# Hybrid state-space and attention encoder on one core: sine arguments in the front, scan outputs through ScalarE, scan input products in pairs

## The chip, the cores and the metric
One core of a Trainium2 chip runs the whole program in one launch. The metric is device time in microseconds. The kernel before takes 1440.96 us, the median of 3 runs (1439.4 to 1441.56).

## What is computed
Two layers over 256 tokens of width 1024, all in float32:

```python
h = rmsnorm(x, g_mix); u, q, k, v = split(h @ w_in)
y_ssm = ssm_mixer(u)          # bidirectional complex-diagonal scan, GELU, GLU, norm
y_att = diff_attention(q, k, v)   # 4 heads, two softmax maps per head
x = x + concat(y_ssm, y_att) @ w_out
h = rmsnorm(x, g_ffn)
x = x + swiglu(h)             # layer 0: dense; layer 1: top 2 of 8 experts
```

The scan part: 32 channel groups with 64 complex states each, forward and backward. A state update is `s[t] = lam * s[t-1] + b(u[t])` with complex `lam`; the output is the real part of `C s`.

## The kernel before
A layer is a front (norm, projection of `u`, tables of the scan), 22 steps in which the scan and the attention run side by side, and an end (gates, output projection, norm). Then come the weights' passes: dense in layer 0, the experts in layer 1, streamed from HBM.

**The scan.** Each of 16 steps i handles two channel groups on 128 partitions. The complex decay is split: its size goes into a real scan, its angle into a rotation before and one after. TensorE makes the input products (`bu`, L1883 to L1892: four products with 64 rows each, rows 0 to 63 for even steps and 64 to 127 for odd ones) into a PSUM bank. VectorE rotates them by cosines and sines (`rotate_in`, L1300 and L1302; `add_in`, L1309) and scans (L1321). GpSimd rotates back (three operations, L646 to L651, into `ro`, two steps deep) and TensorE sums over the states (`outputs`, L1905 to L1924, once for two steps) into `ps[:, 2 + ft % 2]`. Four steps fill one such sum.

**Angles.** ScalarE multiplies positions by the turn of a step and, for the cosine, adds a quarter (`phases`, L729 and L730, four activations of 128 columns); adds a large constant to round (`nearest`, L739); VectorE subtracts the whole turns (`fracs`, L1274); ScalarE takes three sines (`trigs`, L746 to L750). This is done for each step, two steps ahead. `trig` is three steps deep and freed by GpSimd (`products`).

**GELU.** VectorE copies a finished sum, squares, scales and multiplies it (`gelu_in`, L1281 to L1284), ScalarE takes tanh (L756), VectorE closes (`gelu_out`, L1289), reading the sum in PSUM.

**Attention.** Head h starts at step 6, 8, 10, 12. At its step TensorE makes two score maps; one step later VectorE takes minima over rows and scales them (`score`, L1331 and L1332) and ScalarE takes the exponentials with their sums (L768). Two steps later VectorE takes reciprocals (`sums`, L1338 and L1339), ahead of that step's rotation. Three steps later ScalarE puts them on diagonals (L779) and at step +4 TensorE turns the maps (L1956); at +5 it makes the head's output (L1963), which ScalarE empties (L789, L790). Head pairs are normed on VectorE (`head_norm`, L1345 and L1346) and then projected (L1978).

**Order.** Each engine's list is written out by hand per step. TensorE in step i: `bu(i+1)`, the projections of q, k, v (L1863 at steps 0, 1, 3, 4; L2016 at 6 and 8), the attention work, then `outputs`. ScalarE in step i: phases of i+2, sines of i+1, emptying, attention, tanh. Sine, exponential with tanh, and square root need different activation tables, loaded by `ACT_TABLE_LOAD`.

## Time and profile before

| | |
|---|---|
| median of 3 runs | 1440.96 us |
| span of the profiled execution | 1437.0 us (no other time is given for it) |
| TensorE busy | 1348.0 us (94%) |
| VectorE busy | 875.8 us (61%) |
| ScalarE busy | 694.7 us (48%) |
| GpSimd busy | 135.4 us (9%) |

Layer 0's mixer runs from the start to about 200 us, its dense part to 387 us, layer 1's mixer to about 574 us, the experts to the end. A timeline line gives start, length, engine, line of the kernel, operation, tiles and shapes, and in brackets the idle time before it with what ended it. A TensorE product in float32 has two records.

### The profile page before, as it was taken

Reading aid. Unit: us, or ns where it says so; the run is one execution under the profiler, and the core shown is the slowest. Engines: PE = TensorE matmul, PEld = TensorE weight load, DVE = VectorE, ACT = ScalarE, POOL = GpSimd, SP = SyncE. Lnnn points to the kernel's source line nnn. Section 1 sums busy time; section 2 is a strip of 40 time slices with the busy share of each in tenths; the row PEclk is TensorE's granted clock in tenths of the full one; section 3 lists DMA queues with packets and bytes.
Section 4 is the critical chain, followed back from the end, with each engine's and each line's share of the span. In section 5 each row is a group of like instructions: output and inputs, shape, how many; then the busy total and the mean of one; then the engine's idle time right before and its main releaser. Section 6 shows DMA issues by size and latency. Waiting matters only on the chain.

```text
span 1437.0 us, 19125 instructions
## 1 busy us (share of the span) xinstructions
PE 1348.0 (94%) x7246; PEld 980.9 (68%) x7246; DVE 875.8 (61%) x1138; ACT 694.7 (48%) x1023; POOL 135.4 (9%) x111
## 2 busy tenths in 40 slices
PE   6996889999899779899999999999999999999996
PEld 6865558888787555776766667676766666666663
DVE  6888754454398875666565665555665555665552
ACT  4568443434246863445454544454444444444442
POOL 0455200000006640000000000000000000000000
PEclk9997999999899889899999999999999999999999
DMA  8541325443643126699999999999999999999993
GB/s 347 173 171 34 126 106 215 177 175 124 265 125 117 63 66 236 258 411 390 410 421 421 421 421 419 410 421 422 420 422 421 408 420 421 421 421 420 421 421 164
DMA packets 66329, 435.58 MB, mean 303 GB/s; under 512 B 8192, under 2 KB 14720, under 8 KB 16576
## 3 DMA queue, kind: packets, MB, share of 16 engines
q1 hardware_dynamic: 64848, 429.60, 74.4%
q0 software_dynamic: 1392, 4.78, 1.0%
q8 instruction: 57, 0.93, 0.3%
q14 instruction: 32, 0.26, 0.0%
HBM read 429.11 MB, written 2.10 MB: 300 GB/s over the span
## 4 chain that ended last, share of the span: by engine, by line
PE 73%; DMA 9%; DVE 9%; ACT 5%; SPq 2%; issue 2%; ACTq 0%; DVEq 0%
PE ps L2208 19%; PE ps L2243 11%; PE ps L2194 9%; PE ps L2096 7%; PE ps L1863 6%; PE ps L2225 6%; PE ps L2075 4%; DMA raw<-wmoe 4%; DMA first_ring<-wmoe 4%; PE ps L2001 2%; PE ps L1978 2%; SPq L548 2%; DVE raw L1321 1%; PE ps L1901 1%; PE ps L1989 1%
## 5 line engine op out<-in xcount | busy, mean ns | idle before, releaser
L2096 PE MATMUL ps<-wsplit,xh 128*128 128x512 f32 (+1 forms) x352 | 111.4, 388 | 5.0 <-DVE hv L1388 3.4
L1398 DVE TENSOR_TENSOR low_raw<-raw,last_uppers 128x2048 fp32r<-128x2048 f32 x39 | 89.2, 2289 | 38.5 <-ACT last_uppers L839 38.5
L1398 DVE TENSOR_TENSOR low_first<-first_ring,first_uppers 128x2048 fp32r<-128x2048 f32 x31 | 70.8, 2291 | 37.8 <-ACT first_uppers L839 37.8
L2243 PE MATMUL ps<-raw,hn 128*64 128x256 f32 x784 | 92.4, 382 | 0.0
L1863 PE MATMUL ps<-hT,mixw 128*128 128x256 f32 x384 | 89.4, 394 | 3.1 <-DMA mixw<-wmix 2.2
L1398 DVE TENSOR_TENSOR low_raw<-raw,first_uppers 128x2048 fp32r<-128x2048 f32 x31 | 70.8, 2289 | 32.6 <-ACT first_uppers L839 32.6
L1668 DVE TENSOR_TENSOR hv<-hv,ps 128x256 f32<-128x256 f32 x56 | 23.6, 421 | 105.3 <-ACT hv L989 105.3
L1362 DVE TENSOR_TENSOR wsplit<-raw,wsplit 128x2048 fp32r<-128x2048 f32 x33 | 74.5, 2289 | 20.1 <-ACT wsplit L798 20.1
L1863 PEld LDWEIGHTS ps<-hT,mixw 128*128 128x128 f32 x384 | 75.0, 198 | 15.2 <-issue 2.5
L2243 PE MATMUL ps<-last_ring,hn 128*64 128x256 f32 x704 | 83.2, 382 | 0.0
L989 ACT ACTIVATE hv<-ps 128x256 f32<-128x256 f32 x56 | 21.5, 384 | 127.5 <-PE ps L2208 127.5
L646 POOL TENSOR_TENSOR raw<-raw,trig 128x512 f32<-128x512 f32 x32 | 43.5, 1359 | 401.9 <-DVE raw L1321 330.4
L839 ACT ACTIVATE last_uppers<-raw 128x2048 fp32r<-128x2048 f32 x39 | 74.2, 1907 | 11.0 <-DMA raw<-wmoe 11.0
L2208 PE MATMUL ps<-first_uppers,tokens_next 128*128 128x512 f32 x240 | 77.5, 404 | 2.0 <-DVE low_first L1398 2.0
L2096 PEld LDWEIGHTS ps<-wsplit,xh 128*128 128x128 f32 x352 | 65.9, 188 | 17.9 <-DVE wsplit L1362 3.8
L982 ACT ACTIVATE hv<-ps 128x128 f32<-128x128 f32 x56 | 15.5, 277 | 127.2 <-PE ps L2257 127.2
L2243 PEld LDWEIGHTS ps<-raw,hn 128*64 128x64 f32 x784 | 54.0, 137 | 33.5 <-issue 8.8
L2208 PE MATMUL ps<-last_uppers,tokens_first 128*128 128x512 f32 x232 | 74.8, 404 | 0.2 <-DVE low_raw L1398 0.2
L2208 PE MATMUL ps<-last_uppers,tokens_next 128*128 128x512 f32 x208 | 68.4, 411 | 1.9 <-DVE low_raw L1398 1.9
L2208 PE MATMUL ps<-first_uppers,tokens_first 128*128 128x512 f32 x216 | 69.7, 404 | 0.0
L2243 PEld LDWEIGHTS ps<-last_ring,hn 128*64 128x64 f32 x704 | 48.7, 137 | 29.8 <-issue 7.4
L839 ACT ACTIVATE first_uppers<-raw 128x2048 fp32r<-128x2048 f32 x31 | 58.9, 1908 | 18.4 <-DMA raw<-wmoe 16.2
(352 smaller groups left out, 3013.0 us busy)
## 6 DMA issues: line engine op xcount, KB each, us to landing
raw<-wmoe SPq DMA_DIRECT2D x148, 1024.0 KB, 22.4
first_ring<-wmoe SPq DMA_DIRECT2D x95, 1024.0 KB, 23.4
last_ring<-wmoe SPq DMA_DIRECT2D x91, 1024.0 KB, 23.2
raw<-wdense SPq DMA_DIRECT2D x33, 1024.0 KB, 5.0
mixw<-wmix SPq DMA_DIRECT2D x12, 2048.0 KB, 8.3
cyt<-bmat SPq DMA_DIRECT2D x2, 2048.0 KB, 12.1
cw<-cmat SPq DMA_DIRECT2D x2, 2048.0 KB, 18.4
qk<-wglu SPq DMA_DIRECT2D x2, 1024.0 KB, 5.0
```

Source lines behind the costliest of these rows:

```text
L548: sp.dma_start(ring[at], src).then_inc(ring_full[at], 16)
L646: nc.gpsimd.tensor_tensor(ro[:, b, 0], st[:, n % 3], trig[:, n % 3, 0:1, :].to_broadcast([P, 2, SEQ]), ALU.mult)
L839: nc.scalar.activation(uppers[k % UPPERS], ring[at], ACT.Copy).then_inc(s["hi_done"], 1)
L1362: tt(wl[slot], raw[:, PLACE[slot]], wh[slot].bitcast(F32), ALU.subtract).then_inc(s["lo_done"], 1)
L1398: tt(lows[at], ring[at], uppers[k % UPPERS].bitcast(F32), ALU.subtract).then_inc(s["lo_done"], 1)
L1863: ins = mm(ps[:, bank(u), j * 256:j * 256 + 256], mixw[:, c % 2, f, n * P:(n + 1) * P], hT[:, f, :], start=(f == 0), stop=(f == KT - 1))
L2075: ins = mm(ps[:, 2 + 2 * t + n], x2[rows, a, t * P:(t + 1) * P], w2[slot][rows, at:at + 512], start=first and a == 0 and i == 0, stop=last ...
L2096: ins = mm(to, x2[:, fx, t * P:(t + 1) * P], of, start=(fx == 0 and i == 0), stop=(fx == KT - 1 and i == 2))
L2194: ins = mm(ps[:, 2 + n], x2[:, a, 0:P], w2[:, at:at + 512], start=(x == 0 and a == 0 and i == 0), stop=(x == NC_E - 1 and a == 1 and i == 2))
L2208: ins = mm(ps[:, gate_bank(c)], xheavy[m % 2][:, k, fx], w2[:, f * 512:(f + 1) * 512], start=(fx == 0 and i == 0), stop=(fx == KT - 1 and ...
L2225: ins = mm(ps[LCAP * q:LCAP * q + LCAP, 4 + n], lhid[:, q], part[:, at:at + 512], start=(x == 0), stop=(x == NC_E - 1), tile_position=(0, ...
L2243: ins = mm(to, xlight[:, m % 2, fx], of[:, :, q * P:(q + 1) * P], start=(fx == 0), stop=(fx == KT - 1), tile_position=(0, LCAP * q))
```

## The change
It moves the sine arguments of a layer into four blocks of 4, 4, 3 and 5 steps. ScalarE makes them from positions, in the front, and the cosine now comes from the same argument: absolute value, then a sine with a bias of a quarter turn. A head's `sums` stand behind the scan of their step, `score` has one scaling for both maps, and small scalings are tensor products instead of `tensor_scalar`. ScalarE copies and squares a finished sum (`take_y`), which is in one PSUM bank now, and GELU on VectorE reads only SBUF. `bu_pair` makes the input products of two steps, alternating between row halves, into three banks. The exponentials' table is called for ahead of the wait for the scores. Three arguments' tiles share memory with `v`, `hn` and `qk`, so ScalarE waits for `frac_ready` at steps 1 and 2 and for `trig_ready` before `v` and the first exponentials.

```diff
+TURN_STEPS = (4, 4, 3, 5)
...
-        phase = sb("phase", [P, 2, SEQ])
-        turns = sb("turns", [P, 2, 2, SEQ])
+        late = sb("late", [P, 5, SEQ])
...
+        turn_parts = (v[:].rearrange("p t n -> p (t n)"), hn[:, 0], hn[:, 1, 0:3 * SEQ],
+                      late[:].rearrange("p i t -> p (i t)"))
...
+            def phases(l, b):
...
+                for i in range(first, first + TURN_STEPS[b]):
+                    for d in range(2):
+                        ins = nc.scalar.activation(turns_of(i)[:, d * NCH:(d + 1) * NCH], cst[:, C_T:C_T + NCH], ACT.Copy,
+                                                   scale=small[:, 4, 2 * i + d:2 * i + d + 1])
...
+                nc.scalar.activation(trig[:, n % 3, 0], turns_of(i), ACT.Abs).then_inc(s["act_chain"], 1)
+                nc.scalar.activation(trig[:, n % 3, 1], turns_of(i), ACT.Sin, scale=-TWOPI)
+                nc.scalar.activation(trig[:, n % 3, 2], turns_of(i), ACT.Sin, scale=TWOPI)
+                act.wait_ge(s["act_chain"], chain[0])
+                nc.scalar.activation(trig[:, n % 3, 0], trig[:, n % 3, 0], ACT.Sin, bias=col[:, 16:17],
+                                     scale=-TWOPI).then_inc(s["trig_ready"], 1)
+
+            def take_y(l, ft):
+
+                act.wait_ge(s["c_done"], GP * l + 4 * (ft + 1))
+                nc.scalar.activation(yt[:, ft], y_sum, ACT.Copy)
+                nc.scalar.activation(th[:, ft], y_sum, ACT.Square).then_inc(s["y_taken"], 1)
...
+                    nc.scalar.activation(col[:, 89:90], col[:, 17:18], ACT.Exp)
+                    act.wait_ge(s["score_ready"], HEADS * l + h + 1)
...
                 phases(l, 0)
+                phases(l, 1)
                 nearest(l, 0)
                 for k in range(2):
+                    if k:
+                        nearest(l, 1)
+                        phases(l, 2)
+                        phases(l, 3)
...
+                    if i % 4 == 1 and 1 < i < GP + 2:
+                        take_y(l, i // 4 - 1)
...
+                link(stt(th[:, ft], th[:, ft], 0.044715, yt[:, ft], ALU.mult, ALU.mult))
+                tt(th[:, ft], th[:, ft], yt[:, ft], ALU.add).then_inc(s["gin"], 1)
...
+                tt(col[:, c:c + 4], col[:, 34:38], col[:, 24 + h:25 + h].to_broadcast([P, 4]), ALU.mult).then_inc(s["score_ready"], 1)
...
                 turn_b(l)
+                fracs(l, 0)
                 fold_c(l)
...
-                fracs(l, 0)
                 fracs(l, 1)
+                fracs(l, 2)
...
-                    for h in range(HEADS):
-                        if i == HEAD_AT[h] + T_SUMS:
-                            sums(l, h)
                     if i < GP:
                         rotate_in(l, i)
                         add_in(l, i)
                         scan(l, i)
-                    if i + 2 < GP:
-                        fracs(l, i + 2)
+                    for h in range(HEADS):
+                        if i == HEAD_AT[h] + T_SUMS:
+                            sums(l, h)
+                    if i == 1:
+                        fracs(l, 3)
...
-            def bu(l, i):
+            def bu_pair(l, i):
...
+                        for b in range(2):
+                            q = 64 * b
+                            u = ush[q:q + 64, k, NCH:0:-1] if d else ush[q:q + 64, k, 0:NCH]
+                            ins = mm(ps[:, scan_bank(n + b), c:c + NCH], bw[q:q + 64, k, r, d, :], u, start=True, stop=True,
+                                     tile_position=(q, 0))
...
-                if i % 4 == 0 and FT * l + ft >= 2:
-                    pe.wait_ge(s["g_ready"], FT * l + ft - 1)
-                mm(ps[:, 2 + ft % 2, c:c + NCH], loc[:, k, :], usw[:, k, :], start=True, stop=False)
+                if i % 4 == 0 and FT * l + ft:
+                    pe.wait_ge(s["y_taken"], FT * l + ft)
+                mm(y_sum[:, c:c + NCH], loc[:, k, :], usw[:, k, :], start=True, stop=False)
...
-                    if 0 < i < GP - 1:
-                        bu(l, i + 1)
+                    if i % 2 and i < GP - 1:
+                        bu_pair(l, i + 1)
```

ScalarE in layer 0 between the exponentials of head 1 (`hn`) and step 11's sines, before:

```order
L768 ACT_TABLE_LOAD
L768 ACTIVATE hn,col<-ps,col 128x256 x4
L779 ACTIVATE hT<-cst,col 128x128 x4
L756 ACTIVATE cyt<-cyt 128x256
L729 ACTIVATE phase<-cst,small 128x128
L730 ACTIVATE phase<-cst,col,small 128x128
L729 ACTIVATE phase<-cst,small 128x128
L730 ACTIVATE phase<-cst,col,small 128x128
L746 ACT_TABLE_LOAD
L746 ACTIVATE trig<-turns 128x256
L739 ACTIVATE turns<-phase 128x512
L749 ACTIVATE trig<-turns 128x256
```

and after:

```order
L777 ACTIVATE cyt<-ps 128x256
L778 ACTIVATE cyt<-ps 128x256
L792 ACT_TABLE_LOAD
L792 ACTIVATE col<-col 128x1
L798 ACTIVATE hn,col<-ps,col 128x256 x4
L809 ACTIVATE hT<-cst,col 128x128 x4
L783 ACTIVATE cyt<-cyt 128x256
L767 ACTIVATE trig<-late 128x256
L768 ACT_TABLE_LOAD
L768 ACTIVATE trig<-late 128x256
L769 ACTIVATE trig<-late 128x256
L771 ACTIVATE trig<-trig,col 128x256
```

The five activations of 128 and 512 columns are gone, one of 256 is added to the sines, and the two that take the sum stand ahead of the exponentials.

VectorE in layer 0, steps 7 and 8, before (`col` holds minima, scales and sums):

```order
L1274 SCALAR_TENSOR_TENSOR turns<-turns,phase 128x512
L1331 TENSOR_REDUCE col<-ps 128x2
L1332 TENSOR_SCALAR col<-col 128x2
L1331 TENSOR_REDUCE col<-ps 128x2
L1332 TENSOR_SCALAR col<-col 128x2
L1338 RECIPROCAL col<-col 128x4
L1339 TENSOR_SCALAR col<-col 128x2
L1300 TENSOR_TENSOR raw<-ps,trig 128x512
```

and after:

```order
L1369 TENSOR_REDUCE col<-ps 128x2 x2
L1372 TENSOR_TENSOR col<-col 128x4
L1337 TENSOR_TENSOR raw<-ps,trig 128x512
L1339 TENSOR_TENSOR ps<-ps,trig 128x512
L1346 TENSOR_TENSOR ps<-ps,raw 128x512
L1358 SCALAR_TENSOR_TENSOR raw<-small,ps 128x128 x4
L1378 RECIPROCAL col<-col 128x4
L1379 TENSOR_TENSOR col<-col 128x2
```

The subtraction of whole turns is gone, and the reciprocals, which wait for the exponentials, are behind the scan instead of ahead of the rotation.

## Rows read from the trace of the kernel before

**Rows 1.** Cores: span and mean granted TensorE clock.
```profile
core 0: 1437.0 us, clock 0.977
```

**Rows 2.** Busy time by stretch; last columns TensorE clock, DMA share, GB/s.
```profile
core 0: us, PE busy (x) PEld busy (x) DVE busy (x) ACT busy (x) POOL busy (x), PEclk, DMA share, GB/s
...
79.60:151.30 71.70, 55.37 (x331) 40.81 (x329) 63.64 (x119) 57.02 (x142) 43.52 (x34) 0.88 0.23 79
...
457.80:530.00 72.20, 55.92 (x330) 41.11 (x328) 64.24 (x119) 56.97 (x142) 43.45 (x34) 0.86 0.21 75
```

**Rows 3.** Chain that ended last, both layers: start us, us, what.
```profile
30.77 0.61 ACT uT L864
...
36.45 5.77 DMA ush<-uT
...
151.27 3.67 PE ps L1978 x8
...
422.16 7.31 PE ps L1901 x64
...
530.04 3.67 PE ps L1978 x8
```

**Rows 4.** TensorE timeline, layer 0: start us, us, line, op, [idle before <-releaser].
```profile
42.35 1.68 PE L1890 MATMUL ps<-ush,bw 64*128 64x128 f32 x16 [1.22 <-DMA ush<-uT]
...
51.25 1.16 PE L1890 MATMUL ps<-ush,bw 64*128 64x128 f32 x8
...
60.94 1.09 PE L1921 MATMUL ps<-raw,cw 128*64 128x128 f32 x16
...
79.59 1.71 PE L1890 MATMUL ps<-ush,bw 64*128 64x128 f32 x16
...
99.49 1.04 PE L1937 MATMUL ps<-exact 128*128 128x256 f32 x4
...
101.94 1.09 PE L1921 MATMUL ps<-raw,cw 128*64 128x128 f32 x16
...
124.63 3.59 PE L1956 MATMUL ps<-hT,hn 128*128 128x128 f32 x16 [4.48 <-ACT hT L779]
```

**Rows 5.** VectorE timeline, layer 0, same columns.
```profile
114.57 0.68 DVE L1300 TENSOR_TENSOR raw<-ps,trig 128x512 f32<-128x512 f32 x1
...
128.75 0.69 DVE L1274 SCALAR_TENSOR_TENSOR turns<-turns,phase 128x512 f32<-128x512 f32 x1 [1.49 <-ACT turns L739]
...
129.36 0.69 DVE L1300 TENSOR_TENSOR raw<-ps,trig 128x512 f32<-128x512 f32 x1
...
143.30 0.69 DVE L1300 TENSOR_TENSOR raw<-ps,trig 128x512 f32<-128x512 f32 x1 [0.22 <-ACT trig L750]
...
146.77 3.33 DVE L1345 RECIPROCAL hT<-hT 128x512 f32<-128x512 f32 x1
```

**Rows 6.** ScalarE timeline, layer 0, same columns.
```profile
19.87 0.40 ACT L729 ACTIVATE phase<-cst,small 128x128 f32<-128x128 f32 x1 [1.98 <-DMA cst<-consts]
...
121.40 0.47 ACT L768 ACTIVATE hn<-ps,col 128x256 f32<-128x256 f32 x1
...
123.21 1.27 ACT L779 ACTIVATE hT<-cst,col 128x128 f32<-128x128 f32 x4
...
125.00 0.41 ACT L729 ACTIVATE phase<-cst,small 128x128 f32<-128x128 f32 x1
...
126.48 1.28 ACT L746 ACT_TABLE_LOAD   x1
...
128.10 0.61 ACT L739 ACTIVATE turns<-phase 128x512 f32<-128x512 f32 x1
```

**Rows 7.** VectorE groups, 79 to 151 us: busy, mean ns, idle before.
```profile
L1274 DVE SCALAR_TENSOR_TENSOR turns<-turns,phase 128x512 f32<-128x512 f32 x8 | 7.1, 888 | 2.3 <-ACT turns L739 2.3
...
L1332 DVE TENSOR_SCALAR col<-col 128x2 f32<-128x2 f32 x8 | 5.2, 652 | 0.3
```

**Rows 8.** GpSimd group, 79.6 to 151.3 us, same columns.
```profile
L646 POOL TENSOR_TENSOR raw<-raw,trig 128x512 f32<-128x512 f32 x12 | 15.6, 1302 | 36.4 <-PE ps L1921 36.4
```

More of the change, by code:

```diff
@@ L453, in at_least, with turn_part, turns_of @@
                 eng.wait_ge(s[what], n)
+        def turn_part(i):
+            return next(b for b in range(len(TURN_STEPS)) if i < sum(TURN_STEPS[:b + 1]))
+        def turns_of(i):
+            b = turn_part(i)
+            at = (i - sum(TURN_STEPS[:b])) * SEQ
+            return turn_parts[b][:, at:at + SEQ]
         @block.sync
@@ L718, in norm_empty @@
                     ins.then_inc(s["emptied_act"], 1)
-            def phases(l, i):
-                n = GP * l + i
-                act.wait_ge(s["small_dve"], 2 * l + 2)
-                if n:
-                    act.wait_ge(s["frac_ready"], n)
-                for d in range(2):
-                    turn = small[:, 4, 2 * i + d:2 * i + d + 1]
-                    c = slice(d * NCH, (d + 1) * NCH)
-                    nc.scalar.activation(phase[:, 0, c], cst[:, C_T:C_T + NCH], ACT.Copy, scale=turn)
-                    ins = nc.scalar.activation(phase[:, 1, c], cst[:, C_T:C_T + NCH], ACT.Identity, bias=col[:, 17:18],
-                                               scale=turn)
-                chain[0] += 1
-                ins.then_inc(s["act_chain"], 1)
@@ L735, in nearest @@
[L735 to L743 removed]
+            phases_done = {}
+            def phases(l, b):
+                if b == 0:
+                    act.wait_ge(s["small_dve"], 2 * l + 2)
+                first = sum(TURN_STEPS[:b])
+                for i in range(first, first + TURN_STEPS[b]):
+                    for d in range(2):
+                        ins = nc.scalar.activation(turns_of(i)[:, d * NCH:(d + 1) * NCH], cst[:, C_T:C_T + NCH], ACT.Copy,
+                                                   scale=small[:, 4, 2 * i + d:2 * i + d + 1])
+                chain[0] += 1
+                phases_done[b] = chain[0]
+                ins.then_inc(s["act_chain"], 1)
@@ L747, in trigs @@
-                if between:
-                    between()
-                nc.scalar.activation(trig[:, n % 3, 1], turns[:, i % 2, 0], ACT.Sin, scale=-TWOPI)
-                nc.scalar.activation(trig[:, n % 3, 2], turns[:, i % 2, 0], ACT.Sin,
-                                     scale=TWOPI).then_inc(s["trig_ready"], 1)
+                chain[0] += 1
+                nc.scalar.activation(trig[:, n % 3, 0], turns_of(i), ACT.Abs).then_inc(s["act_chain"], 1)
+                nc.scalar.activation(trig[:, n % 3, 1], turns_of(i), ACT.Sin, scale=-TWOPI)
@@ L894, in _ @@
                         else:
+                            act.wait_ge(s["trig_ready"], GP * l + TURN_STEPS[0])
                             nc.scalar.activation(v[:, k - 4], pb, ACT.Copy).then_inc(s["emptied_act"], 1)
```

105 lines of the change are left out of this document (51 added, 54 removed).

## The prediction
> **What bounds the kernel now.** I read the cores first: one span of 1437.0 us at a mean granted clock of 0.977 [rows 1]. The sum below is made against this span. The median of the runs is 1440.96 us, 3.96 us more, which I take as fixed.
>
> Next the busy time by stretch [rows 2]. From 79.60 to 151.30 us TensorE is busy for 55.37 of 71.7 us, VectorE for 63.64, ScalarE for 57.02. Nobody is full, so this is a loop of waits, and layer 1's second row repeats it. Ahead of it TensorE runs without a gap: input products at 42.35, the next at 51.25, and between and behind them local products and projections, with no idle time up to 79.59 [rows 4]. The chain that ended last says what feeds this: `uT` emptied at 30.77 us, the transfer of `ush` from 36.45 for 5.77 us; and what stands behind it: the projection that follows the first head norm, at 151.27 us in layer 0 and at 530.04 us in layer 1 [rows 3]. Behind those two points TensorE has its work waiting. What the mixers gain up to them I carry over to the end whole, since the passes of weights are fed by transfers issued as the work goes.
>
> The loop is read in the timelines, here from rotation 11 (114.57 us) to rotation 13 (129.36) [rows 5], 14.8 us: rotation and scan 3.45, whole turns 0.8, minima and their scaling of one map 1.3, table load 1.28, four exponentials 1.8 (they start at 121.40), diagonals 1.17 and a head's two emptyings 0.62 (both from 123.21 to 125.00), phases 1.48 (to 126.48), table 1.30, one sine 0.32, rounding 0.61 [rows 6], whole turns 0.61, which waited 1.49 us for ScalarE [rows 5]. TensorE stands still meanwhile: 4.48 us ahead of a turn of maps [rows 4].
>
> **The front.** ScalarE's phases begin at 19.87 us, released by a transfer [rows 6]. Ahead of the second `uT` it now makes 32 copies, not 4 or 8 activations. An activation of 128 columns is 0.41 us long, but four with the biased ones fill 1.48 [rows 6]; I take 0.30 for a plain copy, start to start, and 0.9 for a rounding of 1024 columns (0.41 at 128 and 0.61 at 512, continued). So 19.9 + 4.8 + 0.9, `uT` 0.5, 0.9, 4.8 = 31.8 to 32.0: the second emptying is 1.2 us late [rows 3]. At 0.37 each it would be 3.4 us late. `ush` is then awaited until 43.5 instead of 42.2. In layer 1 the wide subtraction delays `fold_c` and so the local products at 422.16 [rows 3] by about 1.1 us.
>
> **Input products.** Sixteen records of two steps took 1.64 us one after another (79.59, 1.71 with its tail), eight took 1.09 with a tail of 1.16 [rows 4]. The sums `outputs` alternate between column halves, and their sixteen take 1.09 us, no longer than eight of the others [rows 4]: halves of the array run beside each other. I take 1.09 us for a pair in row halves; the ends are 0.82 (half of 1.64) and 1.64. The Trainium skill ("TensorE: Matmul & The Clock Gate", part 3 on packing small matmuls by row and column tiling) says that a weight load overlaps only where the row group differs and that such tiles run at once; by it a pair would come near 0.82. No row here shows row halves alternating.
>
> TensorE's list to the sum of steps 6 and 7 then is, from 43.5: five pairs 5.45 (before 1.61 + 4 x 1.08 + 2 x 1.64 = 9.2), the same local products, projections and maps. Before, that sum ended at 102.96 (101.94 and 1.02) [rows 4]. After: 102.96 + 1.15 - 3.75 = **100.35**.
>
> **The step of the first exponentials behind it.** ScalarE takes the sum, 0.75 (two of 256 columns); table 1.3; exponentials 1.84; diagonals 1.17; tanh 0.3; table 1.3 and four passes for the sines 1.3; semaphores 0.1 to 0.3. 100.35 + 8.05 = **108.4** for rotation 11, before 114.57: -6.2. GELU's two products on VectorE, four before, lie beside this; rotation 10 starts at about 103.7 and ends at 107.2.
>
> **A round.** From rotation 11 to 13 go: whole turns 0.8 and 0.61, the table load in the path 1.28 (now called for ahead of the wait), phases 1.48, rounding 0.61. Come: the minima of the second map with one scaling, 0.6, and three passes of ScalarE, 1.0 (absolute value and two sines that the rotation formerly had earlier). 14.8 - 4.8 + 1.6 + 0.2 = **11.8**, so rotation 13 at 120.2. The next round has `take_y` and tanh in it: its sum ends on TensorE at 123.9, behind the turn of the maps (diagonals at 116.9, turn 3.5, maps and sum 3.5, as from 99.49 to 102.96) [rows 4]; take 0.75, table 1.3, exponentials 1.84, diagonals 1.17, head 0.62, tanh 0.3, sines 2.6: rotation 15 at **132.6**, before 143.30 [rows 5]. Scan 3.45, gelu's last product and sums 0.3, reciprocal 3.33 and a product 1.00 (146.77 to 151.27 before) [rows 3, 5]: **140.8** instead of 151.27, **-10.5**.
>
> The sums behind the scan rather than ahead of the rotation cost nothing: the turns they release wait for ScalarE's diagonals in any case. If that cover went, it is 0.4 to 1.5 us a head. Waits for `trig_ready` before `v` and the exponentials are met by ScalarE's own earlier sines. The single PSUM bank for y makes TensorE wait for `take_y`, which comes a step later; its next use is two steps off.
>
> **Layer 1** walks the same way: local products 1.1 late at 423.3, then 96.2 us, as from 44.6 in layer 0, to the projection that stood at 530.04 [rows 3]: 519.5, **-10.5** (-10.0, if the 0.6 us by which layer 1 took longer before stays). Together 21.0: span 1416.0, time **1420.0 us**.
>
> **Neighbours on VectorE.** The subtraction is 0.69 at 128.75, 0.888 in the mean; a scaling of two columns has a mean of 0.652 [rows 7]; GpSimd's operations take 1302 ns [rows 8] and seem to hold some of them up. Traced lengths stand in the sum, so some of this is in it. Without any, another 2 to 3 us fall away.
>
> **Rivals.**
> First: row halves do not overlap, a pair costs 1.64. Five pairs by 0.55 in each layer: +2.75 twice, **1425.5 us**. For it: no row of the trace shows row halves together. Against: column halves do it. 0.20.
>
> Second: VectorE waits for GpSimd. Each new product with two SBUF inputs (GELU's, the scaled minima, sums, 21 in a layer) waits out a GpSimd operation of 1302 ns [rows 8], and four of them stand in the chain from rotation 11 to the norm (two scaled minima, a GELU product, the last sums): 4 x 1.2 = 4.8 in each layer, **1429.6 us**. For it: the means of [rows 7]. Against: a scaling with one input is lengthened there already, so the kinds exchanged may cost alike. The Trainium skill ("SBUF — State Buffer", who interferes with whom) states that a VectorE instruction with two SBUF inputs contends with a GpSimd instruction that reads SBUF and that the loser waits for the whole of it; that rule speaks against this change. By it the whole subtraction would be 1.3 us longer wherever it meets GpSimd; a mean of 0.888 against 0.69 [rows 7] shows it in part at most. 0.09.
>
> Third, the other side: TensorE's clock falls. Between 79.60 and 151.30 it is 0.88 of full, and the turn of maps behind 4.48 us of idleness took 3.59 us for sixteen records, so part of it stood at the lower level of 1.2 GHz; after 1.22 us of idleness at 42.35 it did not fall [rows 2, 4]. The wait for `ush` grows to 2.4. Should the gapless stretch of 35 us from 43.5 to 78.1 run at 1.2 GHz, it doubles: +35 - 21 = 14 over, about **1455 us**. It decides from 21 us of such work at the lower level. Against: the stretch starts as before, with a like idle time. 0.03.
>
> Fourth, that the front does not hide the phases, which is what moving them there is for: at 0.37 each `ush` is 3.4 instead of 1.2 late, and the like in layer 1, 4.4 back, **1424.4 us**. The cover is thin, so 0.05. The rest, 0.03, is spread.
>
> **How the numbers follow.** The forecast has 0.60, at 1420.0, own range 1415 to 1423: lower end with pairs at 0.82 (-1.35 twice) and no neighbour's cost (-2.5), upper end with 0.3 us more in each of ten handovers. The range of 8 in 10 takes in the first rival and most of the second: 1413 to 1430. A measurement of this kernel can tell 0.2%, 3 us. Only the third rival and part of the unforeseen is slower: faster 0.94, same 0.02, slower 0.04.
>
> **What would show it.** Right: pairs of 16 records in about 1.1 us; the second `uT` at 32; rotation 11 at 108 to 109, 13 twelve later; the table load of the exponentials ahead of the last scaling; the norm's projection at 141 and 519. Wrong: scalings above 0.8 us (second rival), pairs at 1.6 (first), a granted clock near 0.5 between 43 and 78 us (third), a wait of rotations for `trig`, or a head's turn that waits for the sums on VectorE.

## The result, and the profile after

The changed kernel takes 1427.66 us, the median of 5 runs from 1424.49 to 1432.22; the kernel before, in the same session, 1441.46 (1439.4 to 1442.35). The ratio is 0.9907, with a 95% interval from 0.9888 to 0.9926. (Here and below, medians leave out runs more than 1.5% above the fastest of the same kernel; that takes two runs away from one kernel.) The change is 13.8 us faster, and the forecast was 21.0 faster: the right side and inside the range of 8 in 10 (1413 to 1430), outside the forecast's own range (1415 to 1423), and the forecast gain was half as large again. Two things stand out at once: the runs spread over 7.7 us, where those of the kernel before spread over 3, and the profiled execution (1424.49 us, span 1422.7) is the fastest of the five.

The cores of the changed kernel, where the kernel before had [rows 1]:

```profile
core 0: 1422.7 us, clock 0.976
```

Its busy time by stretch in layer 0 (columns as in [rows 2]: the stretch and its length, busy time of TensorE, of its weight loads, of VectorE, ScalarE and GpSimd, then TensorE's clock, DMA share, GB/s):

```profile
42.00:47.00 5.00, 4.03 (x41) 3.58 (x39) 4.96 (x5) 1.29 (x2) 0.00 (x0) 0.99 0.26 55
...
47.00:60.00 13.00, 13.00 (x64) 12.30 (x64) 11.31 (x22) 3.27 (x10) 8.74 (x6) 0.50 0.01 1
...
60.00:78.00 18.00, 18.00 (x106) 15.71 (x105) 11.86 (x26) 5.30 (x15) 7.49 (x6) 0.99 0.59 230
```

and the kernel before over all three stretches:

```profile
42.00:79.60 37.60, 37.25 (x245) 32.98 (x245) 28.40 (x55) 23.12 (x63) 16.53 (x12) 1.00 0.46 175
```

The stretch of 47 to 60 us stands at 0.50 of full speed, the level of 1.2 GHz, while TensorE is busy for all of its 13.00 us. In the kernel before the clock stood at 1.00 all the way.

TensorE's timeline of the changed kernel, layer 0 and then layer 1 (start us, length us, line, operation, in brackets the idle time before it with what ended it):

```profile
42.28 1.16 PE L1931 MATMUL ps<-ush,bw 64*128 64x128 f32 x16
...
44.42 11.72 PE L1943 MATMUL ps<-cw,cyt 128*128 128x64 f32 x64 [0.97 <-DVE cw L1296]
...
56.07 2.08 PE L1931 MATMUL ps<-ush,bw 64*128 64x128 f32 x16
...
58.08 8.36 PE L1902 MATMUL ps<-hT,mixw 128*128 128x256 f32 x32
...
66.27 0.38 PE L1954 MATMUL ps<-usw,loc 128*128 128x128 f32 x2
...
105.20 1.09 PE L1963 MATMUL ps<-raw,cw 128*64 128x128 f32 x16
...
147.06 3.24 PE L2020 MATMUL ps<-mixw,cyt 128*128 128x512 f32 x7 [2.10 <-DVE cyt L1387]
...
418.50 1.16 PE L1931 MATMUL ps<-ush,bw 64*128 64x128 f32 x16 [1.28 <-issue]
...
420.46 7.36 PE L1943 MATMUL ps<-cw,cyt 128*128 128x64 f32 x64 [0.80 <-DVE cw L1296]
...
435.85 0.38 PE L1954 MATMUL ps<-usw,loc 128*128 128x128 f32 x2
...
515.56 3.67 PE L2020 MATMUL ps<-mixw,cyt 128*128 128x512 f32 x8 [2.26 <-DVE cyt L1387]
```

The sixteen records of a pair fill 1.09 us (42.28, 1.16 with the tail) where they filled 1.64 [rows 4]. Then comes what the forecast had no price for. The pair starts at 42.28 without any wait for `ush`, where the forecast had a wait until 43.5. The local products (44.42) wait 0.97 us for the folded `cw` and take 11.72 us; in layer 1 the same 64 records wait 0.80 us and take 7.36. The pair behind them takes 2.08, the projection 8.36. The slow stretch costs 4.4 + 0.9 + 1.2 = 6.5 us, and layer 0's norm projection stands at 147.06 us: 4.2 earlier than in [rows 3], not 10.5. Layer 1 has no such stretch: from the first sum of the scan (435.85) to the norm's projection it takes 79.71 us, in layer 0 147.06 - 66.27 = 80.79.

VectorE and ScalarE of the changed kernel between rotation 11 and rotation 15 (L1337 is the rotation, L1372 the scaling of the minima, L792 the call for the exponentials' table, L798 the first exponential):

```profile
107.06 0.93 DVE L1321 SCALAR_TENSOR_TENSOR cyt<-cyt 128x256 f32<-128x256 f32 x1 [0.62 <-ACT cyt L778]
...
108.02 1.37 DVE L1322 TENSOR_TENSOR cyt<-cyt 128x256 f32<-128x256 f32 x1
...
114.60 0.69 DVE L1337 TENSOR_TENSOR raw<-ps,trig 128x512 f32<-128x512 f32 x1 [1.16 <-ACT trig L771]
...
119.35 0.37 DVE L1372 TENSOR_TENSOR col<-col 128x4 f32<-128x4 f32 x1
...
126.26 0.69 DVE L1337 TENSOR_TENSOR raw<-ps,trig 128x512 f32<-128x512 f32 x1 [2.74 <-ACT trig L771]
...
131.02 0.96 DVE L1372 TENSOR_TENSOR col<-col 128x4 f32<-128x4 f32 x1
...
138.81 0.69 DVE L1337 TENSOR_TENSOR raw<-ps,trig 128x512 f32<-128x512 f32 x1 [1.03 <-ACT trig L771]
```

```profile
117.28 1.28 ACT L792 ACT_TABLE_LOAD   x1
...
119.76 0.47 ACT L798 ACTIVATE hn<-ps,col 128x256 f32<-128x256 f32 x1 [0.98 <-DVE col L1372]
```

From rotation 11 to 13 it is 126.26 - 114.60 = 11.66 us, forecast 11.8, before 14.79 [rows 5]; from 13 to 15 12.55, forecast 12.4. In the second profile of the same kernel (a1_changed_again, below) the two are 11.47 and 11.75. The table is loaded at 117.28, ahead of the last scaling (119.35). The steps of the round are as forecast. GELU's two products at 107.06 and 108.02 take 0.93 and 1.37 us, which is the second rival's mechanism, beside the path. One such wait stands in the path: the scaling at 131.02, ahead of head 3's exponentials, takes 0.96 us, in a1_changed_again 0.16, and that is the difference between 12.55 and 11.75.

### The profile page after: what moved, and what is told of

It is laid out like the page before. It is cut to its first block, busy times and chain, and to the rows that moved or that the text cites. A ratio compares the mean times of both kernels' runs of the same rounds, so it can differ in the third digit from the quotient of the medians.

```text
span 1422.7 us, 18990 instructions
## 1 busy us (share of the span) xinstructions
PE 1337.5 (94%) x7246; PEld 970.9 (68%) x7246; DVE 852.9 (60%) x1095; ACT 679.5 (48%) x991; POOL 134.3 (9%) x111
## 4 chain that ended last, share of the span: by engine, by line
PE 74%; DVE 9%; DMA 8%; ACT 5%; SPq 2%; issue 1%; ACTq 0%; DVEq 0%
PE ps L2249 19%; PE ps L2284 11%; PE ps L2235 9%; PE ps L2138 8%; DMA raw<-wmoe 6%; PE ps L2266 6%; PE ps L2117 4%; PE ps L1902 3%; PE ps L2043 2%; PE ps L2058 2%; DMA first_ring<-wmoe 2%; PE ps L2020 2%; SPq L567 2%; PE ps L1943 1%; PE ps L2031 1%
## 5 line engine op out<-in xcount | busy, mean ns | idle before, releaser
L665 POOL TENSOR_TENSOR raw<-raw,trig 128x512 f32<-128x512 f32 x32 | 43.5, 1359 | 387.3 <-DVE raw L1358 324.3
L2138 PE MATMUL ps<-wsplit,xl 128*128 128x512 f32 (+1 forms) x176 | 68.4, 388 | 0.0
## 6 DMA issues: line engine op xcount, KB each, us to landing
cyt<-bmat SPq DMA_DIRECT2D x2, 2048.0 KB, 12.1
```

The source lines that it names most:

```text
L665: nc.gpsimd.tensor_tensor(ro[:, b, 0], st[:, n % 3], trig[:, n % 3, 0:1, :].to_broadcast([P, 2, SEQ]), ALU.mult)
L2138: ins = mm(to, x2[:, fx, t * P:(t + 1) * P], of, start=(fx == 0 and i == 0), stop=(fx == KT - 1 and i == 2))
```

## The experiments

Each kernel is the changed one with one edit, if nothing else is said. For each profile the table has the distance from the first sum of the scan (steps 0 and 1, the `ps<-usw,loc` row at 60.53 us in layer 0 before) to the norm's projection. It measures the loop by itself, free of what the front and the slow stretch do; in the two profiles of the changed kernel it is 79.6 to 80.8 us, and e1_fold_first, whose edit is not in the loop, has 82.23 and 80.83. So up to 2.6 us in it may be scatter.

| kernel | loop, layers 0 and 1, us | wait for folded C, us | slow stretch behind it |
|---|---|---|---|
| before | 90.74, 91.36 | none, none | no, no |
| changed, first profile | 80.79, 79.71 | 0.97, 0.80 | yes, no |
| a1_changed_again | 79.64, 79.66 | 0.91, 0.63 | no, no |
| e1_fold_first | 82.23, 80.83 | 0.38, 1.55 | no, yes |
| e2_halves_apart | 83.40, 81.25 | none, 2.01 | no, yes |
| e3_table_late | 84.02, 83.86 | 0.38, 1.57 | no, yes |
| e4_sums_ahead | 82.25, 81.72 | 0.75, 2.55 | no, yes |
| e6_psum_inputs | 81.23, 79.79 | none, 2.55 | no, yes |
| e7_phases_again | 92.74, 91.77 | 1.00, 1.24 | no, yes |
| e9_before_gap | 91.07, 91.28 | 2.15, 2.74 | yes, yes |

The slow stretch is not equally long in all of them. From the start of the local products to the first sum it takes 15.4 us in the changed kernel without it; with it 21.8 and 21.9 (e3_table_late and the first profile of the changed kernel) to 23.5 (e1_fold_first, e7_phases_again), which is 6.4 to 8.1 us more. In e2_halves_apart it is 9.4 more, in e9_before_gap 9.5 and 9.8.

e5_local_later, e8_together and e10_later_fracs have another order up to the first sum, no such wait and no slow stretch; for them the text gives the distance from the first pair, which is 97.10 and 96.85 us in a1_changed_again.

### Once more, unaltered

> The changed kernel once more, unaltered. In its first profile TensorE's granted clock is 0.50 from about 47 to 60 us, the local products take 11.72 us instead of 7.31, and the norm's projection of layer 0 stands at 147.06 instead of the 140.8 of the walk. Theory A (the fall follows from the list of this kernel: a pair, a gap of about 1 us for the folded C, then work): it is there again at the same place, 147 +- 1. Theory B (it comes and goes from run to run): local products at 7.3 us in this profile, projection at 140 to 142, span about 1416. The times spread from 1424 to 1432 either way if other falls come and go.

1428.18 us (median of 9, 1419.18 to 1433.1), ratio 0.9905 [0.9874, 0.9937]. Its profiled execution was the fastest of the nine, span 1417.4 us:

```profile
42.03 1.16 PE L1931 MATMUL ps<-ush,bw 64*128 64x128 f32 x16
...
44.10 7.36 PE L1943 MATMUL ps<-cw,cyt 128*128 128x64 f32 x64 [0.91 <-DVE cw L1296]
...
139.13 3.67 PE L2020 MATMUL ps<-mixw,cyt 128*128 128x512 f32 x8 [2.18 <-DVE cyt L1387]
...
412.66 7.36 PE L1943 MATMUL ps<-cw,cyt 128*128 128x64 f32 x64 [0.63 <-DVE cw L1296]
...
507.72 3.67 PE L2020 MATMUL ps<-mixw,cyt 128*128 128x512 f32 x8 [2.22 <-DVE cyt L1387]
```

Theory B. With the same list and nearly the same gap (44.10 is behind 0.91 us of idleness), the local products take 7.36 us and no slow stretch follows. The norm's projection stands at 139.13, where the walk of the prediction had 140.8. So the walk holds within 1.7 us for an execution without the slow stretch. That the median is one of executions which mostly have it is argued, not shown: the mean clock of this execution is 0.979, of the other thirteen of the changed kernel 0.971 to 0.977, but only two of the fourteen have a trace.

### VectorE folds C first

```diff
-                fracs(l, 0)
                 fold_c(l)
+                fracs(l, 0)
```

> VectorE folds C ahead of the first wide subtraction again, as in the kernel before; nothing else. The gap of 0.97 us between the first pair and the local products goes (C ready at about 43.2). Theory A (the gap starts the clock's fall in layer 0): local products take 7.3 us, the norm's projection of layer 0 stands at 140 to 141.5, the time is 6 us below the changed kernel's. Theory B (the fall has nothing to do with the gap): the fall stays or moves, gain 0 to 1 us in layer 0. Both: layer 1 gains about 0.8 us or nothing.

1429.97 us (6 runs, 1419.6 to 1432.95), ratio 0.9889 [0.984, 0.9938]: no better than the changed kernel, as theory B had it. In its profile layer 0 is free of the slow stretch, as theory A had it, with the norm's projection at 141.06, and layer 1 has it. The first line is VectorE's, the others TensorE's:

```profile
29.83 2.29 DVE L1291 TENSOR_TENSOR raw<-cw,fold 128x2048 f32<-128x2048 f32 x1 [1.00 <-DMA cw<-cmat]
...
402.72 3.89 PE L1916 MATMUL ps<-cst,cyt 128*128 128x128 f32 x32 [1.25 <-DVE cyt L1281]
...
413.59 1.16 PE L1931 MATMUL ps<-ush,bw 64*128 64x128 f32 x16
...
416.30 13.28 PE L1943 MATMUL ps<-cw,cyt 128*128 128x64 f32 x64 [1.55 <-DVE cw L1296]
```

Layer 0 does not show what the edit brings: the fold there waits 1.00 us for the transfer of C (29.83), about as much as the subtraction would have taken, and e3_table_late, which keeps the subtraction in front, has the same wait of 0.38 us before its local products (at 43.05, here 43.44). VectorE came to this place about 0.6 us earlier than in a1_changed_again.

Layer 1 shows why the edit is not enough. TensorE reached `bt` early (a wait of 1.25 us for VectorE) and the local products early (1.55 us). In this execution TensorE had run at the full clock on the way into layer 1, and in the first profile of the changed kernel it had not:

```profile
385.00:400.00 15.00, 13.09 (x50) 11.23 (x51) 10.84 (x47) 11.37 (x31) 0.00 (x0) 0.67 0.70 295
```

and e1_fold_first:

```profile
385.00:400.00 15.00, 14.02 (x65) 12.16 (x64) 12.07 (x47) 13.40 (x35) 0.00 (x0) 0.96 0.52 221
```

A clock of 0.67 there, 0.96 here; layer 1's front begins some 3 us earlier here, but the same 64 records of its projection take 14.05 us instead of 16.24. A TensorE that reaches the pair sooner runs into VectorE's fold of C and stands there longer. It can be sooner for another reason too: in e3_table_late the projection took 16.18 us, but TensorE waited only 0.57 us ahead of the pair (1.28 in the changed kernel), and then 1.57 for C. The gap is not a constant of the list; it is what is left between two engines. The edit takes about 1.0 us out of it: e4_sums_ahead and e6_psum_inputs, with the same 14.05 us of projection, had 2.55 there. The loop of layer 0 came out 2.6 us longer than in a1_changed_again; a turn of maps ran at the lower level in part (116.98 us: 3.49 us for sixteen records, not 2.02), which I take for scatter, since e10_later_fracs has it too (3.38).

### Halves one after the other

```diff
-                for d in range(2):
-                    for r in range(2):
-                        c = r * SEQ + d * NCH
-                        for b in range(2):
+                for b in range(2):
+                    for d in range(2):
+                        for r in range(2):
+                            c = r * SEQ + d * NCH
```

> The sixteen records of a pair are issued as eight of the upper row half and then eight of the lower, in the same banks with the same waits. Theory A (alternation lets the halves run together): a pair costs 1.6 us instead of 1.09, 5 pairs until the sum of steps 6 and 7: +2.7 us in each layer's norm projection, time +4 to +5.5. Theory B (the gain comes from taking two steps in one place): a pair stays near 1.1 and the time is the same.

```profile
42.13 1.68 PE L1931 MATMUL ps<-ush,bw 64*128 64x128 f32 x16 [0.29 <-DMA ush<-uT]
...
114.20 1.71 PE L1931 MATMUL ps<-ush,bw 64*128 64x128 f32 x16
```

The pair is back at 1.64 us (1.71 with its tail) and the loops take 83.40 and 81.25 us, 3.8 and 1.6 more than in a1_changed_again, on top of two pairs ahead of the first sum, 1.1. 1433.5 us (10 runs, 1422.86 to 1438.67; two more, at 1446.04 and 1447.51, are left out), ratio 0.9924 [0.9887, 0.9961], 5 to 6 us over the changed kernel in the median. Its slow stretch (9.4 us) is part of that. Theory A; with 4.9 and 2.7 a layer its five pairs at 0.55 are met in layer 1, and the rest in layer 0 is within the loop's scatter. The Trainium skill ("TensorE: Matmul & The Clock Gate", part 3 on row and column tiling) says that a weight load overlaps running products only where its row group differs. In blocks neighbouring products have the same row group, alternating they have different ones, and the trace agrees on which is faster: 1.64 and 1.09. A pair in half of 1.64 is not reached: 1.09 against 0.82.

### The table behind the wait

```diff
-                    nc.scalar.activation(col[:, 89:90], col[:, 17:18], ACT.Exp)
```

> The small exponential that calls for the table ahead of the wait for the scores is taken out; the table is loaded with the first exponential behind the wait, as before. Theory A (the call ahead hides 1.28 us wherever ScalarE waited for scores): in layer 0 the exponentials of heads 0, 2 and 3 (they waited 2.28, 0.98 and 1.77 us) start 1.0 to 1.3 later, head 1 (no wait) the same; norm projection +2 to +2.6 in each layer, time +4 to +5. Theory B (the table load is placed by the hardware queue ahead of the wait anyway): same.

1435.91 us (4 runs), ratio 0.9964 [0.9931, 0.9997]. The loops take 84.02 and 83.86 us, 4.4 and 4.2 more than in a1_changed_again, where 2 to 2.6 were expected; against e1_fold_first it is 1.8 and 3.0, so the price is not fixed better than that. The median is 7.7 over that of a1_changed_again. Theory A: ScalarE loads the table only where it meets the first exponential, after the wait. The load in this kernel, then rotation 15 in this kernel and in a1_changed_again (idle time in brackets) show it:

```profile
112.43 1.28 ACT L797 ACT_TABLE_LOAD   x1 [2.24 <-DVE col L1371]
...
134.41 0.69 DVE L1336 TENSOR_TENSOR raw<-ps,trig 128x512 f32<-128x512 f32 x1 [2.31 <-ACT trig L771]
```

```profile
131.03 0.69 DVE L1337 TENSOR_TENSOR raw<-ps,trig 128x512 f32<-128x512 f32 x1 [1.04 <-ACT trig L771]
```

Rotation 13 alone would not show it: it waits 2.80 us here, 1.46 in a1_changed_again, but 2.74 in the first profile of the changed kernel.

### Sums ahead of the rotation

```diff
+                    for h in range(HEADS):
+                        if i == HEAD_AT[h] + T_SUMS:
+                            sums(l, h)
                     if i < GP:
                         rotate_in(l, i)
```

(and gone from behind the scan.)

> The sums of a head stand ahead of the rotation again. Theory A (moved sums cost nothing and bring nothing, since ScalarE's diagonals come later than the scan... in the list): time within 1 us. Theory B (behind the scan they keep VectorE from waiting for the exponentials): at each of heads 0 to 3 the rotation starts later, up to 1 to 2 us a head: at heads 2 and 3 the exponentials end (121.5 and 133.8 us) after that rotation could start (119.6 and 133.65), so +2 us at head 1, +0.2 at head 2 and 3, +2 to +3 in each layer's norm projection.

```profile
116.65 0.18 DVE L1378 RECIPROCAL col<-col 128x4 f32<-128x4 f32 x1 [2.00 <-ACT hn L798]
...
129.33 0.18 DVE L1378 RECIPROCAL col<-col 128x4 f32<-128x4 f32 x1 [0.94 <-ACT hn L798]
```

VectorE waits 2.00 us for head 1's exponentials ahead of rotation 12 (116.65; the rotation starts at 117.13) and 0.94 for head 2's (129.33; the rotation at 130.68). 1430.87 us (10 runs), ratio 0.9922 [0.9896, 0.9948]. The loops are 2.6 and 2.1 us longer than in a1_changed_again, no more than their scatter, and the median is 2.7 us higher, less than its spread. Theory B for the waits, which the rows show; that they cost time is not shown.

### GELU from PSUM

```diff
-                link(stt(th[:, ft], th[:, ft], 0.044715, yt[:, ft], ALU.mult, ALU.mult))
-                tt(th[:, ft], th[:, ft], yt[:, ft], ALU.add).then_inc(s["gin"], 1)
+                link(stt(th[:, ft], th[:, ft], 0.044715, y_sum, ALU.mult, ALU.mult))
+                tt(th[:, ft], th[:, ft], y_sum, ALU.add).then_inc(s["gin"], 1)
...
-                    pe.wait_ge(s["y_taken"], FT * l + ft)
+                    pe.wait_ge(s["gin"], FT * l + ft)
```

> GELU's first two operations on VectorE take the sum from PSUM for one of their inputs instead of the copy in SBUF; the bank is freed by the second of them instead of by ScalarE. Theory A (two SBUF inputs next to GpSimd are held up by one of its operations): 0.93 and 1.37 us beside GpSimd in the changed kernel become 0.42 to 0.45 each; the time gains 0 to 1.5 us, since GELU lies in the path only at rotation 14 or not at all. Theory B (they are long for another reason, the waits on ScalarE or the operation itself): durations stay at 0.9 and 1.37.

VectorE groups of the changed kernel in layer 0, 80 to 147 us (tiles, shapes, count, busy us, mean ns, idle before):

```profile
L1322 DVE TENSOR_TENSOR cyt<-cyt 128x256 f32<-128x256 f32 x3 | 4.1, 1370 | 0.1
...
L1379 DVE TENSOR_TENSOR col<-col 128x2 f32<-128x2 f32 x4 | 0.8, 200 | 0.1
```

and of this kernel:

```profile
L1322 DVE TENSOR_TENSOR cyt<-cyt,ps 128x256 f32<-128x256 f32 x2 | 0.8, 420 | 0.1
...
L1379 DVE TENSOR_TENSOR col<-col 128x2 f32<-128x2 f32 x4 | 2.7, 674 | 0.1
```

The same addition takes 1370 ns with both inputs in SBUF and 420 with one of them in PSUM. The 1.37 us are then its own 0.42 and 0.95 of waiting, less than one operation of GpSimd [rows 8]. Theory A for the mechanism. The Trainium skill ("SBUF — State Buffer", who interferes with whom) says that a VectorE instruction with two SBUF inputs contends with a GpSimd instruction that reads SBUF, and this trace agrees. The time does not follow: 1429.34 us (4 runs), ratio 0.9913 [0.9884, 0.9942], and loops of 81.23 and 79.79 us. A wait is seen instead at the next operation with two SBUF inputs (L1379, the sums' product, now 674 ns, 200 in the changed kernel).

### The phases' load put back

Per step ScalarE makes four activations of 64 columns and one of 256, VectorE one subtraction of 256 columns, and the next sines wait for it. The results are not used. Cut to its core:

```diff
+                    if i + 2 < GP:
+                        phases_again(l, i + 2)
                     if i + 1 < GP:
+                        if i >= 1:
+                            act.wait_ge(s["again_ready"], (GP - 2) * l + i)
                         trigs(l, i + 1)
+                    if i + 2 < GP:
+                        nearest_again(l, i + 2)
...
+                    if i + 2 < GP:
+                        dve.wait_ge(s["again_copied"], (GP - 2) * l + i + 1)
+                        stt(again[:], again[:], ROUND, again[:], ALU.subtract,
+                            ALU.subtract).then_inc(s["again_ready"], 1)
```

> The load that was moved into the front is put back into the steps beside the new scheme, in part: per step ScalarE makes four activations of 64 columns and one of 256, VectorE one subtraction of 256 columns behind the scan, and the next step's sines wait for it; its results are not used. Theory A (the loop from 11 to 13 is closed through ScalarE and these operations): each round from rotation 9 on grows by 2 x 1.0 to 1.4 us where both steps' phases stand in the path, or 1.4 to 2.5 a round, the norm's projection comes 5 to 8 us later in each layer, time +10 to +16. Theory B (ScalarE's removed work had been beside other waits): under 2 us a layer.

1454.51 us (4 runs, 1450.17 to 1456.09), ratio 1.0083 [1.0053, 1.0113]: slower than the kernel before. The loops take 92.74 and 91.77 us, 13.1 and 12.1 more than in a1_changed_again and 2.0 and 0.4 more than before. Theory A, with a larger price than expected (5 to 8 a layer); why it is larger is open. The loops' whole gain over the kernel before was 11.1 and 11.7 us, so with this load put back nothing of it is left: in the loop the phases are the larger part of what the change brings. That the rest cannot pay while they are there is a reading, not shown: this load is not the old one (its shapes are smaller), and the new absolute value and sine stand beside it.

### Local products behind the second projection

```diff
-ZQKV_AT = (0, 1, 3, 4, 6, 8)
-LOCAL_AT = 0
+ZQKV_AT = (0, 1, 2, 4, 6, 8)
+LOCAL_AT = 1
...
-            if k == 0:
+            if k == LOCAL_AT:
...
-                    if i % 2 and i < GP - 1:
+                    if i % 2 and 1 < i < GP - 1:
                         bu_pair(l, i + 1)
...
                                 bu_pair(l, 0)
+                            elif stage == "zqkv1":
+                                bu_pair(l, 2)
```

> TensorE makes the second projection (zqkv1) and the pair of steps 2 and 3 ahead of the local products, and the third projection (zqkv2) ahead of the first outputs, so that nothing waits for the folded C any more (it is ready at 44.4, the local products now come at about 51.6 in layer 0). In five profiles of the changed kernel and its neighbours the clock fell at the local products in one layer four times, behind gaps of 0.97, 1.55, 2.07 and 2.55 us. Theory A (the gap opens the door): no fall between the first pair and the sum of steps 0 and 1 in either layer, norm projections at 139 +- 1 in layer 0, times near the lowest of the changed kernel's, median 1419 to 1423 instead of 1428, and a narrower spread. Theory B (falls come at any place at random, or from the array's load of the first pairs): a fall of 13 us is seen in this stretch again or elsewhere in a gapless stretch, median stays 1427 to 1430.

1420.94 us (5 runs, 1419.11 to 1425.07), ratio 0.9862 [0.9835, 0.9889]. Theory A on all counts but two: layer 0's norm projection stands at 140.41 (139 +- 1 was expected), and a wait of 1.01 us is left in layer 1 for the scan of step 0 ahead of the second pair. No slow stretch follows in either layer, and from the first pair to the norm's projection it takes 97.24 and 99.37 us.

### The later subtractions behind steps 0 and 1

On top of the last:

```diff
-                fracs(l, 1)
-                fracs(l, 2)
                 stack = Stack(None)
...
-                    if i == 1:
-                        fracs(l, 3)
+                    if i == 0:
+                        fracs(l, 1)
+                    if i == 1:
+                        fracs(l, 2)
+                        fracs(l, 3)
```

> As e5_local_later, and VectorE takes the second to fourth wide subtraction behind steps 0 and 1 instead of ahead of step 0. In e5 TensorE waited 1.01 us in layer 1 for the scan of step 0 ahead of the second pair. Theory A (that wait and the clock's risk with it go): the second pair starts without a wait, 0.5 to 1 us a layer, median 1418 to 1420. Theory B (the sines of step 4 now come too late, since their subtraction is later): rotation 4 waits for ScalarE, no gain or up to 2 us lost.

```profile
47.00:60.00 13.00, 13.00 (x103) 12.06 (x102) 12.79 (x22) 6.64 (x17) 10.37 (x6) 1.00 0.57 218
```

```profile
43.31 1.16 PE L1932 MATMUL ps<-ush,bw 64*128 64x128 f32 x16 [1.25 <-DMA ush<-uT]
...
51.51 1.16 PE L1932 MATMUL ps<-ush,bw 64*128 64x128 f32 x16
...
52.60 7.36 PE L1944 MATMUL ps<-cw,cyt 128*128 128x64 f32 x64
...
140.50 3.67 PE L2021 MATMUL ps<-mixw,cyt 128*128 128x512 f32 x8 [2.33 <-DVE cyt L1387]
...
412.96 1.16 PE L1932 MATMUL ps<-ush,bw 64*128 64x128 f32 x16
...
422.25 7.36 PE L1944 MATMUL ps<-cw,cyt 128*128 128x64 f32 x64
...
509.90 3.67 PE L2021 MATMUL ps<-mixw,cyt 128*128 128x512 f32 x8 [2.03 <-DVE cyt L1387]
```

1418.21 us, six runs within 2 us (1416.54 to 1418.51), ratio 0.982 [0.9784, 0.9856]. Theory A. It beats both kernels: 9.5 us under the changed one, 23.8 under the one before. The second pair follows without a wait in both layers, and from the first pair to the norm's projection it takes 97.19 and 96.94 us; the gain over e5_local_later is all in layer 1 (99.37 there). Without the slow stretch a1_changed_again had 97.10 and 96.85. So the gain over the changed kernel is that of the slow stretch: the best run of the changed kernel (1419.18) was nearly there, its median was not.

### The two together

Both edits above, and GELU from PSUM.

> As e10_later_fracs, with GELU's first two operations reading PSUM as in e6_psum_inputs. Theory A (what lies beside the path is worth nothing): within 1 us of e10_later_fracs. Theory B (the 1.4 us that GELU no longer waits for GpSimd shows in rotations 10 and 14): 1 to 2 us less.

1419.13 us (6 runs, 1415.98 to 1421.45), ratio 0.9825 [0.9788, 0.9863], 97.28 and 96.96 us from the first pair. Theory A: what lies beside the path brings nothing.

### A gap put into the kernel before

```diff
+                link(tt(ctmp[:, 0], c[0], f(1), ALU.mult))
                 tt(ctmp[:, 0], c[0], f(1), ALU.mult)
```

> The kernel before, with the first product of the fold of C made twice (2.2 us more on VectorE, the same values). C is then ready at about 45.5 instead of 43.3 in layer 0 and 2.2 us later in layer 1, so TensorE waits about 1.6 and 2.1 us between the first input products and the local products, where it did not wait at all. Theory A (a gap of 1 to 2.5 us at this place lets the clock fall, and a fall costs about 6.5 us): the profile has a granted clock near 0.5 for 13 us behind at least one of the two gaps, and the median rises by the gaps, 3 to 4 us, and by falls, 5 to 13 us: 1449 to 1458. Theory B (falls belong to the changed kernel alone, say to its row halves): no fall here, median 1444 to 1445.

```profile
42.19 1.68 PE L1891 MATMUL ps<-ush,bw 64*128 64x128 f32 x16 [1.11 <-DMA ush<-uT]
...
46.03 13.91 PE L1902 MATMUL ps<-cw,cyt 128*128 128x64 f32 x64 [2.15 <-DVE cw L1255]
...
437.84 13.71 PE L1902 MATMUL ps<-cw,cyt 128*128 128x64 f32 x64 [2.74 <-DVE cw L1255]
```

and by stretch (columns as in [rows 2]):

```profile
46.00:66.00 20.00, 19.97 (x82) 18.83 (x83) 14.93 (x30) 12.14 (x34) 8.29 (x6) 0.50 0.00 1
```

1463.84 us (6 runs, 1455.99 to 1467.1), ratio 1.0131 [1.0089, 1.0172]. One operation of 2.2 us, whose result was there already, costs 22 us. The gaps are 2.15 and 2.74 us, the local products take 13.91 and 13.71 instead of 7.36, while the loops stay at 91.07 and 91.28. Theory A, beyond its price: the range of the expectation ended at 17. The sum closes: the slow stretch lasts 20 us here, so from the local products to the first sum it takes 26.08 and 26.34 us instead of 16.57 twice, 9.5 and 9.8 more; with the gaps that is 24.2, and the spans differ by 1462.2 - 1437.0 = 25.2. This kernel has neither alternating row halves nor anything else of the change, so the slow stretch needs nothing of the change. That the gap brings it is shown by adding the gap here and by taking it away in e10_later_fracs.

## Why the prediction was right, and where it was not

**Input products.** 1.09 us for a pair, taken from the column halves of `outputs`, is what the rows after show in every pair at the full clock (2.08 us at the lower level). Taken apart again it costs 2.7 to 4.9 us a layer, where the first rival had 2.75.

**The sum of steps 6 and 7.** Forecast to end at 100.35; in the first profile it ended at 106.2 (105.20 and its 1.02), late by 5.9 us, where the slow stretch accounts for 6.5. In a1_changed_again, without that stretch, it ended at 99.44, the local products began at 44.10 (walk: 44.6) and the norm's projection at 139.13 (walk: 140.8). The local products' time was right for another reason than the walk's: it had TensorE wait for `ush` until 43.5, and none for C in layer 0. The second `uT` was emptied at 32.06, as forecast, but `ush` was there when the pair started (42.28 and 42.03), and the wait was for C. That these two came out alike is luck.

**The round.** 11.8 and 12.4 forecast, 11.66 and 12.55 measured, 11.47 and 11.75 in a1_changed_again. This was the heart of the sum.

**The sums behind the scan.** "Cost nothing" is right for the step as it is now. What it did not say is what they bring: without it rotation 12 waits 2.00 us; the loop is 2.1 to 2.6 us longer, which is no more than scatter. The walk of the new list had it without naming it.

**Layer 1.** The distance from local products to the norm's projection was to be 96.2 us, and is 507.72 - 412.66 = 95.06 without a slow stretch. (The projection "at 519" left out that layer 0's gain shifts layer 1; against the shifted start it is 509, and a1_changed_again has 507.72.) Both layers together gain 22.3 us up to there, 21.0 forecast. In this 22.3, 2.5 us are already given back in the stretch that I took over whole: between layer 0's norm projection and layer 1's first pair it took 269.2 us before and 271.7 in a1_changed_again, of which the front's later `ush` was forecast. From layer 1's norm projection to the end another 2.7 are given back (907.0 before, 909.7 in a1_changed_again), so the spans differ by 19.6: 1417.4, where 1416.0 was forecast.

**The step that failed** is the sentence on the wide subtraction: that it "delays `fold_c` and so the local products at 422.16 by about 1.1 us". As a delay it is right: from the first product of `turn_b` on VectorE to the folded C it takes 22.1 us in layer 1 with the subtraction in front and 21.1 without (e1_fold_first). In layer 0, for which the walk had no delay, C was ready at 44.40 instead of 43.34. As a price it is wrong, since it and the shorter pair (0.55) open a gap on TensorE where there had been none, and behind a gap there the clock may fall. The third rival had the right mechanism, with the wrong place, size and chance. It looked at the wait for `ush`, which was to grow to 2.4 us and was not there at all in layer 0; it had the whole stretch of 35 us slow, where 13 us were (up to 20 in other kernels); and it had 0.03, where seven of the eight profiles of the changed kernel and its variants with the local products in their old place show it in one layer (a1_changed_again is the exception). Priced as measured, 6.4 to 9.4 us in one layer in seven profiles of eight, 6.8 in the mean, the forecast would have been about 1427 (an estimate, since six of the eight are of variants).

The range of 8 in 10 was drawn to 1430 for the first two rivals. Neither came, and 1427.66 lies in it because of a mechanism that had 0.03: that the range held is luck.

Of the 7.7 us by which 1427.66 lies above 1420.0, a slow stretch of the first profile's size would have 6.5; the run of 1427.66 has no trace, and the profiled one took 1424.49. The rest is within what the weights' passes vary by: from layer 1's norm projection to the end it took between 905.0 us (e4_sums_ahead) and 911.0 (e5_local_later) in the thirteen profiles, though these passes are the same.

**GpSimd's neighbours.** The second rival's price of 4.8 us a layer did not show. The waits are there (1370 ns instead of 420), but most stand where VectorE had time, and with GELU's removed the time stayed. Of the four that the rival put in the chain, one is seen in it, for 0.8 us in the first profile (131.02) and not in a1_changed_again.

**What is not settled.** Why 0.97 us of idleness let the clock fall in one execution and not in another is open. The table holds twelve places with a wait of 1.00 us or none before the local products, with one slow stretch behind them, and eight with 1.24 to 2.74 us, each with a slow stretch. Yet TensorE also waited 1.22 us ahead of the first input products before [rows 4], 1.25 in e10_later_fracs, and 1.28 and 1.49 in layer 1 of the two profiles of the changed kernel, and kept its clock: the wait behind the short pair is not like the wait ahead of it, and no run tells why. Seven of the eight long waits are in layer 1, so layer and wait are parted by e9_before_gap alone. e5_local_later and e10_later_fracs put a projection between the pair and the local products as well as taking the wait away; that their standing next to each other does it without a wait is spoken against by the four places with no wait, of before, e2_halves_apart and e6_psum_inputs.

The kernel before has rare longer executions too: 7 of the 46 runs of it that were made beside the experiments took 1448 us or more (at most 1456.41, mean clock 0.967 to 0.970), the others 1437.4 to 1443.3. None of the 7 has a trace, so whether the clock can fall there without a gap at this place is not known.

## What to carry to other kernels

A small gap in a long dense stretch of TensorE can cost many times its own length (0.97 us of waiting and 6.5 us behind it; 4.9 us and 22 in e9_before_gap), so an operation that is put ahead of another on a feeding engine has to be priced against the slack that TensorE has there, and the best use of a reordering may be to give the late input something to hide behind. If the runs of a kernel spread more than those of its predecessor, profile it again before looking for the reason in one trace. And walk the closed loop of waits, operation by operation: it gave the length of a round to 0.15 us in one profile and to 0.65 in the other.

## What was not expected of the hardware

- A slow stretch of 13 to 20 us at the level of 1.2 GHz in the middle of uninterrupted work: 47.00 to 60.00 us with TensorE busy for 13.00 us at a clock of 0.50 in the changed kernel, 46.00 to 66.00 in e9_before_gap. In the changed kernel it began some 2 us after the gap, not in it (42 to 47 us: 0.99), and it ended while the work went on. In one and the same list it came in layer 0 in one execution and in neither layer in another.
- Alternating row halves take 1.09 us for sixteen records of 64 rows, where eight take the same and sixteen in blocks take 1.64.
- Two SBUF inputs on VectorE cost an addition of 256 columns 1370 ns beside GpSimd, one 420.
